# A two-layer hybrid trunk with mixture-of-experts layers on one core: one-hot transposes and additions ahead of the last pair of experts, an expert's loads in halves, another order in the last norm

## The reference

```python
def hier_moe(h, router_group, router_expert, w_gate, w_up, w_down):
    g_prob = softmax(xt @ router_group)          # 4 groups, top 1
    e_sel = (xt @ router_expert)[chosen group]   # 8 experts, top 2
    gate = g_gate * softmax(e_val)
    ...
    hb = silu(xb @ w_gate[e]) * (xb @ w_up[e])   # xb: the tokens of expert e
    y = hb @ w_down[e]                           # w_gate, w_up: 1024x512, w_down: 512x1024
    # y is weighted by gate and added to its tokens

def reference(...):
    h = x
    for layer in range(2):
        h = h + mixer(rms_norm(h, norm_mix_g[layer]))
        h = h + hier_moe(rms_norm(h, norm_ffn_g[layer]), ...)
    return rms_norm(h, norm_final_g)
```

## Time and profile before

| | us |
|---|---|
| median of 3 runs | 1640.63 |
| lowest and highest | 1638.78, 1641.99 |
| the profiled execution, its own time | 1641.0 |
| its span, first to last instruction | 1639.3 |
| TensorE busy | 1590.3 (97%) |
| VectorE, ScalarE, GpSimd busy | 562.4, 347.5, 214.6 |
| TensorE's granted clock, mean | 0.993 |

### The profile page before, as it was taken

The page is one execution under the profiler, slowest core; times in us unless marked ns, Lnnn a source line. Parts: engine busy times, 40 slices in busy tenths (PEclk is TensorE's granted clock), DMA queues, the critical chain, the costliest instruction groups (busy, mean ns, idle before and its releaser), DMA issues.

```text
span 1639.3 us, 18354 instructions
## 1 busy us (share of the span) xinstructions
PE 1590.3 (97%) x7304; PEld 808.7 (49%) x7304; DVE 562.4 (34%) x1286; ACT 347.5 (21%) x579; POOL 214.6 (13%) x255
## 2 busy tenths in 40 slices
PE   7999999999999999988999999999999999999987
PEld 4444556444444444423766666656544444444422
DVE  4222735232222222125244444435432222222125
ACT  3132611100000000013444444432010000000013
POOL 5000000000000000000344444420000000000002
PEclk9999999999999999999999999999999999999999
DMA  8611074999999999993511112114699999999995
GB/s 314 240 52 52 27 297 165 411 425 427 427 428 426 427 427 427 427 421 132 206 52 52 52 58 79 71 44 170 276 425 428 427 426 427 429 426 428 426 427 216
DMA packets 55304, 471.07 MB, mean 287 GB/s; under 512 B 12334, under 2 KB 12342, under 8 KB 29616
## 3 DMA queue, kind: packets, MB, share of 16 engines
q1 hardware_dynamic: 50592, 462.51, 68.0%
q0 software_dynamic: 4480, 7.29, 1.2%
q10 hardware_dynamic: 144, 0.05, 0.0%
HBM read 452.03 MB, written 23.35 MB: 290 GB/s over the span
## 4 chain that ended last, share of the span: by engine, by line
PE 93%; DVE 4%; issue 1%; ACT 1%; DMA 0%; POOLq 0%; DVEq 0%; ACTq 0%
PE ps L766 27%; PE ps L781 14%; PE ps L657 12%; PE ps L978 10%; PE ps L674 8%; PE ps L571 5%; PE ps L974 3%; PE ps L993 3%; PE ps L643 2%; PE ps L772 1%; DVE sb_h L1916 1%; PE ps L623 1%; PE ps L900 1%; PE ps L690 1%; PE ps L701 1%
## 5 line engine op out<-in xcount | busy, mean ns | idle before, releaser
L766 PE MATMUL ps<-sb_ring,sb_work 128*56 128x512 f32 x2048 | 455.8, 597 | 14.1 <-issue 14.1
L766 PEld LDWEIGHTS ps<-sb_ring,sb_work 128*56 128x56 f32 x2048 | 140.6, 131 | 315.2 <-issue 315.1
L781 PE MATMUL ps<-sb_ring,sb_work 128*56 128x512 f32 x1024 | 233.2, 597 | 0.0
L657 PE MATMUL ps<-sb_work,sb_h 128*128 128x224 f32 x896 | 199.4, 366 | 0.0
L1386 POOL DMA_INDIRECT expert_rows<-sb_work,sb_ri x56 | 51.3, 915 | 1080.0 <-DVE sb_work L1801 684.1
L1773 DVE TENSOR_TENSOR sb_work<-sb_work,ps 56x512 f32<-56x512 f32 x64 | 68.3, 1067 | 357.8 <-ACT sb_work L1208 357.8
L657 PEld LDWEIGHTS ps<-sb_work,sb_h 128*128 128x128 f32 x896 | 160.4, 189 | 47.7 <-issue 44.2
L978 PE MATMUL ps<-sb_work,sb_ring 128*128 128x512 f32 x384 | 168.5, 592 | 1.6 <-DVE sb_work L1502 1.6
L781 PEld LDWEIGHTS ps<-sb_ring,sb_work 128*56 128x56 f32 x1024 | 64.7, 129 | 130.4 <-issue 130.2
L1208 ACT ACTIVATE sb_work<-ps 56x512 f32<-56x512 f32 x64 | 37.7, 589 | 424.4 <-PE ps L766 424.4
L1216 ACT ACTIVATE sb_work<-ps 56x512 f32<-56x512 f32 x56 | 33.1, 591 | 383.0 <-PE ps L781 383.0
(11 more groups left out here) (242 smaller groups left out, 1389.5 us busy)
## 6 DMA issues: line engine op xcount, KB each, us to landing
sb_ring<-in_w_gate_dram SPq DMA_DIRECT2D x64, 2048.0 KB, 18.8
sb_ring<-in_w_up_dram SPq DMA_DIRECT2D x64, 2048.0 KB, 22.7
sb_ring<-in_w_down_dram SPq DMA_DIRECT2D x64, 2048.0 KB, 22.1
sb_ring<-in_c_w_in_dram SPq DMA_DIRECT2D x8, 2048.0 KB, 8.2
sb_ring<-in_ab_w_in_dram SPq DMA_DIRECT2D x5, 2048.0 KB, 11.3
expert_rows<-sb_work SPq DMA_DIRECT2D x2, 4096.0 KB, 20.4
sb_ring<-expert_rows SPq DMA_DIRECT2D x8, 1024.0 KB, 32.2
sb_ring<-in_ab_w_out_dram SPq DMA_DIRECT2D x2, 2048.0 KB, 7.8
```

Of the source, the lines that this page charges most:

```text
L657: mm = nc.tensor.matmul(bank(job)[:, (c % 2) * PICK * CAP:(c % 2 + 1) * PICK * CAP], h_cols(t, c), me["sel"][:, t, 0:PICK * CAP], start=(i ...
L766: mm = nc.tensor.matmul(dst[64 * z:64 * z + CAP, :], me["xgT"][:, j, c, q * CAP:(q + 1) * CAP], wblock(slots[z], NC)[:, c, :], start=(c == ...
L781: mm = nc.tensor.matmul(dst[64 * z:64 * z + CAP, :], src[:, c * CAP:(c + 1) * CAP], wblock(slots[2], FC)[:, c, z * 512:(z + 1) * 512], sta ...
```

## The change

- **Loads in halves.** Gate and up of expert 3 are loaded in two halves of 8 KB per partition (line 480 of the changed kernel). The first halves are issued when half of expert 0's gate/up matmuls are done (a new semaphore `gu_half`), the second ones when all are.
- **One-hots earlier.** VectorE makes them right behind expert a's turned copy. They lie in row buffer 0 now, free once the even experts' scatters have landed, and VectorE waits for that.
- **Transposes and additions.** TensorE transposes the one-hots and adds the first pair to tiles 0 and 1 behind b's down matmuls; the gate/up matmuls of c follow in one piece.
- **Tile 0's turn in layer 0** leaves its place between the additions; all four tiles are turned behind `add_rows`. ScalarE's order is as it was.
- **Last norm.** GpSimd no longer multiplies; it rearranges the final gains when b's gate/up is done. The gains are loaded at the end of mixer C, over the masks that only mixer C needs (`tables`). VectorE multiplies tile 0 and half of tile 3, and for tiles 1, 2 and the other half does gain and root in one instruction. Its order of combining, adding and scaling changes.

```diff
@@ -101,8 +101,9 @@
         gkey = sb("gkey", [P, NG])
         ekey = sb("ekey", [P, NE])
         tokval = sb("tokval", [P, 2, NT])
-        masks = sb("masks", [P, LEVELS, P])
-        keep = sb("keep", [P, T])
+        tables = sb("tables", [P, LEVELS * P + T])
+        masks = tables[:, 0:LEVELS * P].rearrange("p (a b) -> p a b", a=LEVELS)
+        keep = tables[:, LEVELS * P:]
@@ -193,13 +194,13 @@
...
-        fin_g = ring[:, 0, 0:D]
+        fin_g = tables[:, 0:D]
...
         junk2 = me["sel"].rearrange("p a b -> p (a b)")
-        late_sel = junk2.rearrange("p (i t s) -> p i t s", i=PAIRS, t=NT)
+        late_sel = me["rows"][:, 0, :].rearrange("p (i t s) -> p i t s", i=PAIRS, t=NT)
@@ -369,7 +371,9 @@
...
             for e in range(NE):
                 e_in.append([])
-                for s in EXPERT_SLOTS[e % 3]:
+                for part, s in enumerate(EXPERT_SLOTS[e % 3]):
+                    if e == 3 and part < 2:
+                        loads[s] += 1
                     place(e_in[-1], s)
@@ -460,12 +464,24 @@
                     sp.wait_ge(y_ready, HEADS_C)
                     weight_load(l, 1, 0)
                     weight_load(l, 1, 1)
+                    sp.dma_start(fin_g, final_g[None, :].broadcast_to([P, D])).then_inc(final_in, 16)
...
-                for e in range(3, NS):
+                for half in range(2):
+                    if half == 0:
+                        sp.wait_ge(gu_half, l + 1)
+                    else:
+                        wait_full(sp, ("gu", l, 0))
+                    for part, w in enumerate((w_gate, w_up)):
+                        s, n = EXPERT_SLOTS[0][part], SLOT // 2
+                        sp.dma_start(ring[:, s, half * n:(half + 1) * n],
+                                     by_partition(w[l, 3:4])[:, half * n:(half + 1) * n]).then_inc(ring_in[s], 16)
+                wait_full(sp, ("dn", l, 0))
+                weight_load(l, 3, 2)
+                for e in range(4, NS):
                     wait_full(sp, ("gu", l, e - 3))
                     weight_load(l, e, 0)
                     weight_load(l, e, 1)
@@ -525,7 +541,6 @@
             moe_loads(1)
             more_loads(1)
             rows_back(1)
-            sp.dma_start(fin_g, final_g[None, :].broadcast_to([P, D])).then_inc(final_in, 16)
             for t in range(NT):
                 sp.wait_ge(out_ready[t], 1 if t < NT - 1 else 2)
                 sp.dma_start(out[0, t * P:(t + 1) * P, :], xh2[:, t, :]).then_inc(out_stored, 16)
@@ -804,6 +819,8 @@
                     for b in range(4):
                         wait_drained(pe, ("pick", l, 0, b))
                         mm = gate_up(l, three, 0, 0, (2 * b, 2 * b + 1))
+                        if b == 1:
+                            mm.then_inc(gu_half, 1)
@@ -866,12 +883,11 @@
                 last_down(l, a, range(3, 4))
                 last_down(l, b, range(0, 4))
                 more_blocks(l)
-                last_gate_up(l, c, range(0, 6))
                 late_turn(l)
-                last_gate_up(l, c, range(6, 8))
                 late_add(l, 0, 0)
+                late_add(l, 0, 1)
+                last_gate_up(l, c, range(0, 8))
                 last_turn(l, c)
-                late_add(l, 0, 1)
                 last_gate_up(l, d, range(0, 8))
                 last_down(l, c, range(0, 3))
@@ -943,7 +959,7 @@
                             turn_hidden(l).then_inc(o["pe"], 1)
                             pe.wait_ge(o["dve"], n * 4 + 3)
                             down(l, more_slots).then_inc(o["pe"], 1)
-                    pe.wait_ge(o["dve"], NE * per_e * 4)
+                    pe.wait_ge(o["dve"], NE * per_e * 4 + 1)
...
             def moe(l):
                 pick_first(l, 3)
@@ -952,8 +968,6 @@
                 last_experts(l)
                 for t in range(NT - 1):
                     late_add(l, 1, t)
-                if l == 0:
-                    turn_rows(2, range(0, 1))
                 late_add(l, 0, NT - 1)
                 late_add(l, 1, NT - 1)
                 add_rows(l, NT - 1)
...
-            turn_rows(2, range(1, NT))
+            turn_rows(2)
...
             moe(1)
             pool.wait_ge(final_in, 16)
+            wait_full(pool, ("gu", 1, NS + 1))
             g.tensor_copy(fin_c.rearrange("p (c q) -> p c q", c=NC), chunked(fin_g)).then_inc(fin_ready, 1)
-            pool.wait_ge(fin_ready, 1)
-            for t in range(NT - 1):
-                for nb in range(2):
-                    wait_drained(pool, ("add", 1, t, nb))
-                g.tensor_tensor(hg[:, t, :], h[:, t, :], fin_c, ALU.mult).then_inc(hg_ready[t], 1)
@@ -1825,13 +1835,14 @@
                 a, b, c, d = range(NS, NE)
                 last_hidden(l, a)
                 last_turned(l, a)
+                dve.wait_ge(scattered[0], 16 * (l + 1) * (NS // 2))
+                late_selections(l).then_inc(late_ready, 1)
                 last_hidden(l, b)
                 last_turned(l, b)
                 dve.wait_ge(scattered[1], 16 * (l + 1) * (NS // 2))
                 keep_rows(l, a)
                 keep_rows(l, b)
                 more_blocks(l)
-                late_selections(l)
                 for k in range(2):
                     ins = v.tensor_scalar(diag[:, k, :], ident[:], gates[:, k, NT - 1:NT], None, ALU.mult)
                 ins.then_inc(late_ready, 1)
...
+                return ins
...
+                    dve.wait_ge(o["scatter"], NE * per_e * 16)
+                    late_selections(l).then_inc(o["dve"], 1)
...
             def final_rows(t, first):
 
                 n = slice(first, NC)
+                wide = lambda row: row.rearrange("p (c q) -> p c q", c=NC)[:, n, :]
+                norm_col(4, t)
                 dve.wait_ge(rstd_ready, 4 * NT + t + 1)
-                dve.wait_ge(hg_ready[t], 1)
-                v.tensor_scalar(chunked(xh2[:, t, :])[:, n, :],
-                                hg[:, t, :].rearrange("p (c q) -> p c q", c=NC)[:, n, :],
-                                rstd[:, 4, t:t + 1], None, ALU.mult).then_inc(out_ready[t], 1)
+                v.scalar_tensor_tensor(out=chunked(xh2[:, t, :])[:, n, :], in0=wide(h[:, t, :]),
+                                       scalar=rstd[:, 4, t:t + 1], in1=wide(fin_c), op0=ALU.mult, op1=ALU.mult
+                                       ).then_inc(out_ready[t], 1)
+
+            def weigh(t, n):
+
+                for nb in range(2):
+                    wait_drained(dve, ("add", 1, t, nb))
+                dve.wait_ge(fin_ready, 1)
+                v.tensor_tensor(hg[:, t, 0:n], h[:, t, 0:n], fin_c[:, 0:n], ALU.mult).then_inc(hg_ready[t], 1)
...
                 combine(l, 1)
                 add_late(l, 0)
                 add_late(l, 1)
-                norm_col(2 * l + 2, 0)
                 if l == 0:
+                    norm_col(2, 0)
                     norm_rows(2, 0)
-                combine(l, 2)
-                norm_col(2 * l + 2, 1)
-                if l == 0:
+                    combine(l, 2)
+                    norm_col(2, 1)
                     norm_rows(2, 1)
-                add_late(l, 2)
-                add_late(l, 3)
-                if l == 0:
+                    add_late(l, 2)
+                    add_late(l, 3)
                     for t in (2, 3):
                         norm_col(2, t)
                         norm_rows(2, t)
                     for t in (2, 3):
                         turned_rows(2, t)
                 else:
-                    for nb in range(2):
-                        wait_drained(dve, ("add", l, NT - 1, nb))
-                    dve.wait_ge(fin_ready, 1)
-                    v.tensor_tensor(hg[:, NT - 1, :], h[:, NT - 1, :], fin_c, ALU.mult).then_inc(hg_ready[NT - 1], 1)
+                    weigh(0, D)
+                    combine(l, 2)
+                    norm_col(4, 0)
                     final_rows(1, 0)
-                    norm_col(4, 2)
+                    add_late(l, 2)
+                    add_late(l, 3)
+                    weigh(3, D // 2)
                     final_rows(2, 0)
-                    norm_col(4, 3)
                     final_rows(3, NC // 2)
```

8 lines of the change are left out of this document (4 added, 4 removed).

## The result

The changed kernel takes 1633.57 us (median of 7 runs, 1632.49 to 1635.49) against 1640.63 before; the ratio is 0.9959, 95% interval 0.9947 to 0.9970. It is faster by 7.1 us. The forecast was 14.6 us faster, 1626.0, and the time lies above its range (1622.5 to 1632.5): the sign was right, half of the gain is missing.

What follows compares the result with a forecast made beforehand. TensorE was taken to bound the loop and the weights the start of c. From the profiled 1641.0 us, 7.7 (layer 0) and 6.9 (layer 1) came off: 1626.4; the median, 0.4 lower, gave 1626.0, range 1622.5 to 1632.5.

Steps and rivals of the forecast that it cites:

- the weights bound the start of c: Before c's gate/up in each layer: TensorE idles 6.23 us (layer 0) and 5.53 us (layer 1), waiting for c's weights.
- TensorE pays only at c: DMA stream through the expert loop: it falls behind some 0.8 us per expert, but TensorE waits for it only at c.
- Part 1: Expert 3's loads: halves start 3.4 us earlier, but expert 4's issue cuts the gain to 0.5 (layer 1) and 1 us (layer 0).
- Part 2: Transposes and adds moved into the idle piece before c: saves 4.9 us in layer 1 and 5.8 us in layer 0.
- c starts at 1586.6: Layer 1: b's copy, four transposes and eight adds just fit the idle piece, so c starts at 1586.6, against 1586.5.
- Part 3: GpSimd's copy of final gains in layer 1: costs 0 to 1.2 us, 0.6 taken, 0.3 of it swallowed by d's weights.
- Part 4: End of layer 1: 3.6 us instead of 5.9 behind the last adds, saving 2.3 us.
- Part 5: End of layer 0, tile 0's turn behind the adds: saves 9.2 us, less 1.5 for the clock, so 7.7.
- A: Idle piece before c: the fill does not hold the clock, 2.4 or 3.5 us per layer lost; 1630.8 to 1633, chance 0.17.
- B: Layer 0's end: only transposes run about 10 us, mixer C starts at 1.2 GHz; 2.9 us more, 1628.9, chance 0.19.
- C: Before c: transposes or adds wait for another engine, c held 3 us beyond its weights per layer; 1632, chance 0.07.
- D: Expert 3's loads: half-length rows move at a lower rate, making the stream late; 1646 at 0.4 rate, chance 0.04.

Runs made afterwards that it cites:

- e13: The changed kernel executed once more, nothing edited; 1632.37 us (one run).
- e4: The changed kernel without TensorE's branch (`more_blocks`) around the further blocks of experts, untaken with this input; 1631.89 us.
- e6: The changed kernel with ScalarE's squares of tiles 2 and 3 ahead of its copies of tiles 0 and 1 at layer 0's end; 1631.29 us.
- e1: The changed kernel with expert 3's gate and up loaded whole again instead of in halves; 1632.98 us.
- e14: Second execution of the changed kernel with the second pair of adds moved between c's gate/up and its turn; 1631.17 us (one run).
- e10: The changed kernel with GpSimd's copy later, second add behind c's gate/up, ScalarE's squares first, and 14 extra transposes ahead of mixer C; 1624.11 us.
- e2: The kernel before with the halves of expert 3's loads alone; 1640.91 us.

## Why the prediction was wrong

**What bounds the kernel.** Right in the main. TensorE bounds the loop, the weights bounded c. But "the weights bound the start of c" was read as "nothing else is there": the wait of 5.5 us also hid whatever TensorE's own list did behind b, and that was never priced. "TensorE pays only at c" was not right either: in the trace of before it also waited 1.22 and 1.15 us for b's up matrix, and that wait varies by more than a microsecond from one execution to the next.

**Part 1.** The mechanism is right: 8.1 and 8.0 us for expert 4's gate, the halves nearly worthless. The size, 0.5 and 1 us, was still too good for d: in layer 0 d's weights landed at 688.02 + 31.8 = 719.8, less the 0.65 of the start just where they did before. That is 1.0 us of layer 0's miss. c, for its part, started 0.9 us after its weights there (709.05 and 709.96), 5.49 us behind b.

**Part 2, the step that failed.** "c starts at 1586.6" in layer 1, as early as before, was to be 5.6 us behind b. In e13 and e4 it is 5.45, so the sum of copy, transposes and adds was right. It did not hold the branch, which in the trace of before took 0.43 us and stood inside the weight wait. In after's trace c started 7.36 us behind b. Of the 2.4 us missing up to the adds of layer 1, 1.9 is that (7.36 - 5.44) and 0.4 the copy. The saving behind c was right: 9.29 us from c to d, for 14.56. In layer 0, 1.0 of the missing 2.4 us is d's weights and 1.3 the clock at d's start (14.40 to 15.71): the clock stayed up ahead of c, as forecast, but not 10 us later, at the wait that lost its add. I had noted that this add "is now gone from there at no gain"; what it may have done for the clock had no term.

**Part 3.** 1.0 us where 0.6 was taken, inside its bounds and near the upper one. None of it was swallowed by d's weights, since c was late for other reasons.

**Part 4.** 1.76 for 2.3. The mis-sized term is the fused norm: taken as 1.3 behind the last addition (and as 1.6 for tile 1 ahead of it) from the combining step, a form with contiguous rows (2.60/2 in after too), it took 2.06, and it writes its columns in another order. No run takes the two forms apart, so that this order is what costs is a reading.

**Part 5.** 23.67 us from adds to mixer C for a forecast of 24.2, right and a little better. The clock's price was taken as 1.5 and was 2.1. The price of ScalarE's order was right in kind too: e6 takes it back and gains 2.8 to 3.3 us.

**The rivals.** A (the fill does not hold the clock) did not come true in after: 1.00 from 1578 to 1585. At its place it came true in layer 1 of e1, e6 and e14, where the slow branch left a pause of 3.0 to 3.3 us, and one block later, at d, in three passages. B has the right place and a wrong cause: mixer C did start at 1.2 GHz, but through the pause, not through the transposes (e10), and at 2.1 us instead of 4.4. C, c held beyond its weights for something that stands on no other engine's list, is what happened in layer 1, with 3.8 us; I had looked for it on ScalarE and in b's rows, not on TensorE. D is wrong, as e2 shows; its last figure is off as well, since 0.4 of the rate would make the time 1648.6 by its own terms, not 1646.

Counted on the traces, of the 6.1 us by which after's execution missed: 1.9 branch, 1.3 clock at d, 1.0 d's weights in layer 0, 0.6 clock in mixer C, 0.5 fused norm, 0.4 copy, 0.65 the start; against it 0.5 from part 5. These are 5.9. The medians miss by 7.6, and the rest, 1.5, is mostly that the profiled execution was a quick one. How often the branch is slow in unprofiled runs isn't known.

## What to carry to other kernels

Before you fill an idle piece, list what your own engine's queue does inside it, branches and code loading too: the wait that you remove was hiding them, and they come out at full size. Where an engine waits ahead of a long run of matmuls, a few transposes that nobody needs can be worth more than they cost: 14 of them won 1.7 us in the traces here, 2.0 by the medians. Where an add had been moved out of such a wait, the clock fell behind it in 3 of 14 passages. A later look at the order of one engine's list is cheap: ScalarE's squares ahead of its copies, with two other edits of a line each, won about as much (7.5 us by the medians, 6.2 by the ratios) as the whole change.
